# Sparse attention values for two heads at once, and the query norm of cross attention moved into the exponential's scale

## The reference, cut to what matters

```
o_c = softmax(q k_c) v_c                # 31 compressed blocks
o_s = causal_softmax(q k_slc) v_slc     # branch 1
o_w = causal_softmax(q k_win) v_win     # branch 2
o   = g0 * o_c + g1 * o_s + g2 * o_w
```

```
q = rope(rms_norm(p_q, q_norm));  k = rope(rms_norm(p_k, k_norm)), and for the context rms_norm alone
a = softmax(q [k, k_ctx]^T / 8) [v, v_ctx]
rms_norm(x, g) = x / sqrt(mean(x*x) + 1e-6) * g
```

## Time and profile before

| what | value |
| --- | --- |
| median of 3 runs | 3086.56 us (3086.36 to 3092.05) |
| the profiled execution's own time | 3092.79 us |
| its span | 3090.9 us, mean granted TensorE clock 0.952 |
| busy: TensorE, VectorE, ScalarE, GpSimd | 2896.7, 1366.3, 675.4, 1072.2 us |
| the chain that ended last, TensorE's share | 85% (VectorE 5%, DMA 4%) |
| sparse values, L1149 | 640 records, 103.0 us |
| cross attention's scores, L1180 | 128 records, 57.4 us |

### The profile page before, as it was taken

One profiled execution on the slowest core, in us unless ns is written; L12 is line 12 of the kernel. 1 busy time (PEld: TensorE's weight loads), 2 busy tenths in 40 slices (PEclk: granted clock), 3 DMA queues, 4 the chain that ended last, 5 costly groups with the idle time before them and its releaser, 6 DMA issues.

```text
span 3090.9 us, 32580 instructions
## 1 busy us (share of the span) xinstructions
PE 2896.7 (94%) x11791; PEld 1945.3 (63%) x11791; DVE 1366.3 (44%) x2684; ACT 675.4 (22%) x1588; POOL 1072.2 (35%) x574
## 2 busy tenths in 40 slices
PE   7899999999999999998899978989999999999997
PEld 5465544476666644654567546577888544788886
DVE  6333365305455633334655155444355322433464
ACT  2132133123233412323223122111110100211101
POOL 4782583187470007804840000287000583000000
PEclk7999999989999999998898988999999999899998
DMA  7342342253231014312310100254222343122321
GB/s 231 119 126 75 109 126 78 76 154 89 82 89 35 14 55 138 118 61 80 102 47 14 55 14 14 82 158 141 81 92 85 121 152 109 59 91 81 95 86 65
DMA packets 244976, 278.21 MB, mean 90 GB/s; under 512 B 39251, under 2 KB 217696, under 8 KB 244736
## 3 DMA queue, kind: packets, MB, share of 16 engines
q1 hardware_dynamic: 215872, 175.56, 18.6%
q0 software_dynamic: 28224, 100.86, 10.5%
q10 hardware_dynamic: 768, 0.30, 0.0%
HBM read 274.59 MB, written 2.10 MB: 90 GB/s over the span
## 4 chain that ended last, share of the span: by engine, by line
PE 85%; DVE 5%; DMA 4%; issue 2%; ACT 2%; POOL 1%; SPq 1%; DVEq 0%; POOLq 0%; ACTq 0%
PE psum L709 26%; PE psum L1305 24%; PE psum L859 10%; PE psum L845 3%; PE psum L736 3%; PE psum L1149 3%; PE psum L833 2%; PE psum L1135 2%; PE psum L1180 2%; PE psum L751 2%; DMA ring<-in_ffn_w_up 1%; PE psum L983 1%; PE psum L984 1%; DMA ring<-in_ffn_w_gate 1%; ACT probsT L1556 1%
## 5 line engine op out<-in xcount | busy, mean ns | idle before, releaser
L709 PE MATMUL psum<-h,ring 128*128 128x512 f32 (+1 forms) x1808 | 778.5, 589 | 31.7 <-ACT h L1521 24.1
L636 POOL DMA_DIRECT2D ada_ring<-in_ada_w x192 | 114.7, 597 | 1481.6 <-DVE gains L2034 1268.5
L709 PEld LDWEIGHTS psum<-h,ring 128*128 128x128 f32 x1808 | 346.1, 194 | 426.6 <-issue 413.6
L648 POOL TENSOR_SCALAR ada_ring<-ada_ring,cond 128x1024 f32<-128x1024 f32 x168 | 479.6, 2855 | 9.9 <-POOL ada_sum L652 1.8
L652 POOL TENSOR_TENSOR ada_sum<-ada_sum,ada_ring 128x1024 f32<-128x1024 f32 x168 | 398.5, 2372 | 14.9
L859 PE MATMUL psum<-og,ring 128*128 128x512 f32 x768 | 333.2, 593 | 2.3 <-DVE og L2566 2.0
L1305 PE MATMUL psum<-og,arena 128*128 128x256 f32 x1152 | 258.6, 379 | 1.7 <-ACT probs L1872 1.7
L859 PEld LDWEIGHTS psum<-og,ring 128*128 128x128 f32 x768 | 144.6, 190 | 182.0 <-issue 178.5
L1305 PEld LDWEIGHTS psum<-og,arena 128*128 128x128 f32 x1152 | 218.7, 190 | 32.1 <-issue 2.4
L1305 PE MATMUL psum<-h,ring 128*128 128x256 f32 x768 | 180.9, 390 | 4.3 <-ACT h L1521 4.3
L1556 ACT ACTIVATE probsT<-psum 128x128 f32<-128x128 f32 (+3 forms) x232 | 104.3, 450 | 323.6 <-PE psum L833 323.0
(11 more groups left out here) (332 smaller groups left out, 3997.8 us busy)
## 6 DMA issues: line engine op xcount, KB each, us to landing
ada_ring<-in_ada_w POOLq DMA_DIRECT2D x192, 512.0 KB, 4.0
ring<-in_ffn_w_gate SPq DMA_DIRECT2D x22, 1024.0 KB, 5.3
ring<-in_ffn_w_up SPq DMA_DIRECT2D x22, 1024.0 KB, 5.4
ring<-in_ffn_w_down SPq DMA_DIRECT2D x16, 1024.0 KB, 5.0
ring<-in_sc_w_in SPq DMA_DIRECT2D x12, 1024.0 KB, 6.2
ring<-in_mla_w_in SPq DMA_DIRECT2D x10, 1024.0 KB, 6.7
ring<-in_mla_w_out SPq DMA_DIRECT2D x8, 1024.0 KB, 5.1
ring<-in_swa_w_in SPq DMA_DIRECT2D x16, 512.0 KB, 5.2
```

Source lines behind the costliest of these rows:

```text
L636: pool.dma_start(ada_ring[:, i % 2, :], w[k * P:(k + 1) * P, first(part)]).then_inc(arrived[i % 2], n.give(f"ada_in{i % 2}", 16))
L648: step = nc.gpsimd.tensor_scalar(piece, ada_ring[:, i % 2, :], c, None, ALU.mult)
L709: m = pe.matmul(tile.at[:, part], lhs(k), rhs(k), start=(k == 0), stop=(k == K - 1))
```

## The change

Sparse stage: the units' order becomes branch, query block, head. `nsa_v` has 64 columns without zeros, and eight clears of them go. The value step of head 0 only keeps its probability buffer; that of head 1 issues both heads' products, for each key block head 0 and then head 1, each with a 64-column weight and its own half of the output partitions.

Hybrid stage: a query tile is multiplied by the norm's gain twice out of PSUM, once with the cosine (`query_cos`) and once without, for the partner (`take_query`); ScalarE squares the tile in PSUM (`square_query`). TensorE sums the squares with the tokens as rows (`query_sums`), so the sums are 8 columns of 128 partitions; root and reciprocal make them `hy_scale`, with 64 eps in the root, so that the factor 1/8 is in it. It is the scale of the exponential and a factor of the maximum, a column for each unit. The partner of query pair 0 moves ahead of the values, and the wait for the second rotated pair moves into the scores of step 1.

```diff
@@ -218,9 +219,9 @@
-        for e in range(2):
-            for branch in (1, 2):
-                for j in range(TT):
+        for branch in (1, 2):
+            for j in range(TT):
+                for e in range(2):
                     units.append({"branch": branch, "q": j, "head": e, "width": (j + 1) * P, "groups": [(0, (j + 1) * P)],
                                   "opens": False, "first": False, "last": e == 1 and branch == 2 and j == TT - 1,
                                   "blocks": causal_blocks(j), **more})
...
-        nsa_v = [[view(10404 + 1536 * i + 768 * b, TT, 192) for b in range(2)] for i in range(2)]
+        nsa_v = [[view(10404 + 1536 * i + 768 * b, TT, 64) for b in range(2)] for i in range(2)]
...
-                    if u["head"] == 0 and u["branch"] == 1 and u["q"] == 0 and u["pair"] % 2 == 0:
+                    if u["head"] == 0:
+                        first_head.append(pT)
+                        return None
+                    if u["branch"] == 1 and u["q"] == 0 and u["pair"] % 2 == 0:
                         evacuated(value_tiles[kv])
-                    at = 64 - 64 * u["head"]
+                    both = (first_head.pop(), pT)
                     for i, (_, key, q) in enumerate(u["blocks"]):
-                        m = pe.matmul(o[:, q * P:(q + 1) * P], nsa_v[kv % 2][u["branch"] - 1][:, key, at:at + P],
-                                      pT[:, i * P:(i + 1) * P], start=False,
-                                      stop=(u["head"] == 1 and u["branch"] == 2 and i == len(u["blocks"]) - 1),
-                                      skip_group_check=True)
+                        for e in range(2):
+                            m = pe.matmul(o[64 * e:64 * e + 64, q * P:(q + 1) * P], nsa_v[kv % 2][u["branch"] - 1][:, key, :],
+                                          both[e][:, i * P:(i + 1) * P], start=False,
+                                          stop=(u["branch"] == 2 and i == len(u["blocks"]) - 1), skip_group_check=True)
                     return m
...
                 def scores(u, bank):
+                    if u["head"] == 0 and u["q"] == 1:
+                        pe.wait_ge(S["rope_ready"], n.take("rope_ready"))
                     half = slice(64 * (u["head"] % 2), 64 * (u["head"] % 2) + 64)
                     q = hy_q[half, u["head"] // 2, u["q"] * P:(u["q"] + 1) * P]
                     for i in range(2):
...
+                def query_sums(i):
+
+                    tile = next_tile()
+                    pe.wait_ge(S["sq_ready"], n.take("sq_ready"))
+                    squares = sq[:, i, :]
+                    for j in range(TT):
+                        m = pe.matmul(tile.at[:, 2 * j:2 * j + 2], squares[:, j * P:(j + 1) * P], C["ones64"][:, 0:P:64],
+                                      start=True, stop=True)
+                    m.then_inc(S["tile_done"], 1)
...
                     product(w8(open_slot(), 0), h_lat, KT, first_of_slot=True)
-                    head_mean_square(2, lat)
+                    query_sums(0)
+                    partner(2, 1)
                     tokens_tile(open_slot(), 64, range(TT + CT), True)
-                    head_mean_square(3, lat)
-                    partner(2, 2)
-                    partner(3, 1)
-                    for _ in range(3):
+                    query_sums(1)
+                    partner(3, 2)
+                    for _ in range(2):
                         pe.wait_ge(S["rope_ready"], n.take("rope_ready"))
                     attend(units, scores, turned, block_values(lambda u, key: hy_v[:, key, :]), depth=wide)
...
-                        e = nc.scalar.activation(scored, scored, ACT.Exp, bias=neg_max[:, step % 4, g:g + 1], scale=scale,
+                        e = nc.scalar.activation(scored, scored, ACT.Exp, bias=neg_max[:, step % 4, g:g + 1],
+                                                 scale=scale(u) if w > T else scale,
                                                  accum_out=row_sum[:, step % 4, g:g + 1])
...
-                        v = nc.scalar.activation(nsa_v[kv % 2][b][:, :, 64:128],
+                        v = nc.scalar.activation(nsa_v[kv % 2][b],
...
+                def square_query(i):
+                    tile = next_tile()
+                    act.wait_ge(S["head_normed"], n.take("head_normed", 2))
+                    nc.scalar.activation(sq[:, i, :], tile.at, ACT.Square).then_inc(S["sq_ready"], n.give("sq_ready"))
+                    act.wait_ge(S["sq_ready"], n.now("sq_ready"))
+                    act.sem_inc(tile_used[tile.bank], 1)
+
+                def query_root(i):
+                    tile = next_tile()
+                    done(tile)
+                    nc.scalar.activation(hy_scale[:, i, :], tile.at[:, 0:2 * TT], ACT.Sqrt, bias=C["eps64"]
+                                         ).then_inc(tile_used[tile.bank], 1)
...
                     square_head(0, lat)
                     square_head(1, ctx_part)
                     head_rms(0, lat)
-                    square_head(2, lat)
+                    square_query(0)
                     head_rms(1, ctx_part)
                     skip(1)
-                    square_head(3, lat)
-                    head_rms(2, lat)
+                    square_query(1)
+                    query_root(0)
+                    skip(1)
...
-                    head_rms(3, lat)
-                    skip(2)
-                    n.take("head_normed", 2)
-                    attend(units, SCALE64, depth=wide)
+                    query_root(1)
+                    skip(1)
+                    attend(units, lambda u: hy_scale[:, u["head"] // 2, 2 * u["q"] + u["head"] % 2:
+                                                     2 * u["q"] + u["head"] % 2 + 1], depth=wide)
...
-                        nc.vector.tensor_scalar(neg_max[:, b, 0:1], row_max[:, b, 0:1], -scale, None, ALU.mult
+                        nc.vector.tensor_scalar(neg_max[:, b, 0:1], row_max[:, b, 0:1], scale(u), -1.0, ALU.mult, ALU.mult
...
-                        nc.vector.memset(nsa_v[i][b][:, :, 0:64], 0.0)
-                        z = nc.vector.memset(nsa_v[i][b][:, :, 128:192], 0.0)
+                        z = nc.vector.memset(nsa_k[i][b][0:64, 1, :], 0.0)
...
+                def take_query(i):
+
+                    tile = next_tile()
+                    done(tile)
+                    if i:
+                        dve.wait_ge(S["rope_ready"], n.now("rope_ready"))
+                    nc.vector.scalar_tensor_tensor(query_cos[i], tile.at, g_q, C["ax_cos"], ALU.mult, ALU.mult)
+                    nc.vector.tensor_scalar(hy_raw[:, (2 + i) % 3, :], tile.at, g_q, None, ALU.mult
+                                            ).then_inc(S["head_normed"], n.give("head_normed"))
+
+                def query_scale(i):
+
+                    evacuated(next_tile())
+                    nc.vector.reciprocal(hy_scale[:, i, :], hy_scale[:, i, :]).then_inc(S["dve_step"], n.give("dve_step"))
+
+                def turn_query(i):
+
+                    tile = next_tile()
+                    done(tile)
+                    dve.wait_ge(S["dve_step"], n.now("dve_step"))
+                    settle(nc.vector.tensor_tensor(tile.at, tile.at, C["ax_sin"], ALU.mult))
+                    nc.vector.tensor_tensor(hy_q[:, i, :], query_cos[i], tile.at, ALU.add).then_inc(tile_used[tile.bank], 1)
+                    evacuated(tile)
+                    dve.sem_inc(S["rope_ready"], n.give("rope_ready"))
...
                     take_in(0, lat)
                     take_in(1, ctx_part)
                     norm_head(0, lat, g_k)
-                    take_in(2, lat)
+                    take_query(0)
                     norm_head(1, ctx_part, g_k, hy_k[:, T:T + CTX])
                     turn_head(0, hy_k[:, 0:T])
-                    take_in(3, lat)
-                    norm_head(2, lat, g_q)
+                    take_query(1)
+                    query_scale(0)
+                    turn_query(0)
                     skip(1)
-                    norm_head(3, lat, g_q)
-                    turn_head(2, hy_q[:, 0, :])
-                    turn_head(3, hy_q[:, 1, :])
+                    query_scale(1)
+                    turn_query(1)
...
-                    attend(units, SCALE64, None, out, depth=wide)
+                    def scale_of(u):
+                        at = 2 * u["q"] + u["head"] % 2
+                        return hy_scale[:, u["head"] // 2, at:at + 1]
+
+                    attend(units, scale_of, None, out, depth=wide)
```

More of the change, by code:

```diff
@@ L97, in constant_columns @@
         "eps": np.full((P, 1), EPS),
+        "eps64": np.full((P, 1), 64 * EPS),
         "ax_cos": np.cos(ax),
@@ L410, in build @@
         hy_v = view(4352, TT + CT, P)
+        hy_scale = view(5120, 2, 2 * TT)
         ctx_tok = view(8704, CT, D)
@@ L1083, in nsa @@
                     hidden = tile
-                keys, value_tiles = {}, {}
+                keys, value_tiles, first_head = {}, {}, []
```

(11 more changed lines are left out.)

## The result

The changed kernel takes 3071.26 us (median of 20 runs, 3060.34 to 3086.57); the kernel before, over 20 runs, 3092.07 us. The ratio is 0.9933, 95% interval 0.992 to 0.9946: 20.8 us faster. I had forecast 38 us and a range that ended at 3070.

The account below looks back on a forecast made before the run. It took TensorE as the bound in both stages, with a VectorE chain before cross attention's scores; 25.7 us sparse plus 12.7 cross attention, 38 together, gave 3048.6 us, 8-in-10 range 3030 to 3070.

Parts of the forecast that it names:

- The couples: Sparse stage values: two heads' 64-column products overlap in different column halves, 1.14 us saved per branch and pair, 18.2 us.
- The waits: Sparse stage: fewer TensorE waits for copies of transposed probabilities, 0.9 us per eight units without a projection, 7.5 us saved.
- Rival 1: Sparse stage: copies and softmax do not shrink, so waits cost 8 us instead of saving 7.5; 3064 us, chance 0.20.
- The loads: Sparse stage: value copies and loads keep number and order, weight slots open at the same points; no effect.
- The memsets: Sparse stage: eight VectorE memsets removed, worth nothing, since VectorE waits 25.90 us after them.
- The chain before the scores: Cross attention: shorter VectorE work between token projection and first row maximum, saving 5.9 us in turn 2, 7.7 in turn 1.
- The two bank waits: Cross attention, before the token projection: TensorE waits for query tiles' banks, 1.3 us more and 1.1 us.
- The exponential: Cross attention: scale as a column adds 0.09 us in each of 32 strictly serial steps, 2.9 us lost.
- TensorE's clock: Cross attention: with the shorter gap, part of the lower-clock loss goes, 1 us a turn (bounds 0 and 2.7), 2 saved.
- the prediction's own signs of being wrong: Three signs: couples over 0.15 us, copy waits beyond 3 us per eight units, token projection ending more than 6 us later.
- a rival for the sparse stage: No change: the sparse stage idles oftener and TensorE's clock falls in many pairs, 1.7 us a fall; chance 0.04.
- The base: Whole kernel: the median of 3086.56 us from which the 38 us were subtracted to give 3048.6.

Follow-up runs that it names:

- order_only: Kernel before with only the sparse stage's new unit order, old 128-column value weights kept: 3080.16 us, ratio 0.9946.
- busy_all: Changed kernel with thrown-away 512-column products ahead of each early partner product and of each turn's first transposes: 3056.79 us, ratio 0.9876.
- sparse_only: Kernel before with only the sparse stage's part of the change, cross attention as before: 3072.66 us, ratio 0.9923.
- cross_wide: Kernel before with only cross attention's part of the change, query sums over 128 columns instead of 2: 3079.65 us, ratio 0.995.
- late_bank: Kernel with only the sparse part changed, plus two more copies of each query tile before the one freeing its bank: 3095.80 us, ratio 0.9998.
- after_again: The changed kernel once more, unaltered, for a second profile and its spread: 3074.05 us, ratio 0.9926.
- cross_only: Kernel before with only cross attention's part of the change, sparse attention as before: 3099.55 us, ratio 1.001.
- wide_sums: Changed kernel with the query sums over 128 columns (same sums repeated) instead of 2: 3057.52 us, ratio 0.9873.
- serial_halves: Kernel before with only the sparse part, each value step issuing all blocks of head 0, then all of head 1: 3080.78 us, ratio 0.9944.
- after: The changed kernel itself, both parts, against the kernel before: 3071.26 us, ratio 0.9933.
- wide_busy: Changed kernel with 128-column query sums and thrown-away products in TensorE's three waits of each turn: 3055.71 us, ratio 0.9877.

## Why the prediction was wrong, point by point

- **The couples (18.2 us): the mechanism held, the term was too large for the stage.** Eight records take 0.58 us as read from the earlier trace rows. In the last pair the difference to order_only is 13.14 - 11.79 = 1.35 us for eight units, more than the 1.14 that I had priced. Over the stage it is less: 543.4 us in order_only, 530.2 to 532.9 in eight profiles of the full sparse part and 536.8 in a ninth, so 10 to 13 us, and 7 by the ninth. The "up to two-fold" that the prediction quotes from the Trainium skill, page TensorEngine Tiling (Array Packing), stands there in the section Theoretical Speedup; here sixteen records take 1.51 us in one half and 1.02 as couples, with what going in and out costs.
- **The waits (7.5 us): too small for the stage.** The order alone gives 13.5 us of stage, 13.8 in the median. In the last pair it saves only 13.80 - 13.14 = 0.66 us of each eight units, so most of it lies where projections stand between the steps, and there I had put the gain at nothing. Which waits it takes away there is not traced. Couples and waits together were 25.7 us, against 24.0 to 26.8 measured in the stage (20.2 in busy_all): a right sum of two wrong sizes, which is luck. Eight units were forecast at 11.7 us and take 11.79. Rival 1 (the chain takes it back) fell.
- **The loads (nothing): wrong by some 4 us.** The prediction kept the weight loads at nothing because their number and order stay. But the layer behind the sparse stage takes 262.9 to 264.4 us in the four kernels with the old value products, and in the ten with 64-column ones 262.8 and 263.1 us in two and 266.4 to 270.1 in eight (medians 263.8 and 268.0). TensorE comes there earlier and waits for weights, and the 12 records behind the wait are slower too; the layer's mean granted clock is 0.99 before and 0.97 after. Timeline of TensorE, before and then after:

```profile
1222.44 5.42 PE L709 MATMUL psum<-arena,ring 128*128 128x512 f32 x12 [1.17 <-DMA ring<-in_mla_w_q_b]
```

```profile
1206.12 6.94 PE L711 MATMUL psum<-arena,ring 128*128 128x512 f32 x12 [3.54 <-DMA ring<-in_mla_w_q_b]
```

  Of the 24 to 27 us that the sparse stage gains, 21.9 arrive in the median of sparse_only. What sets the time of this load is not traced. The memsets were nothing, as said; no run tested them alone.
- **The chain before the scores (5.9 + 7.7): right where the clock holds.** 4.1 us instead of 3.6 from projection to first maximum. The two bank waits that I priced at 1.3 more and 1.1 us are 1.84 (before 0.44, so 1.4 more) and 1.48. In turn 2 the projection ends 3.7 us later, as forecast (3.6), and 9.0 us are saved behind it: 5.4 us, forecast 5.9. cross_wide, with the chain unchanged, gives 14 to 15 us.
- **The exponential (+2.9): wrong.** The instruction does take 0.09 us more, and by the Trainium skill, page ScalarE: Activation LUTs, section What ACT_TABLE_LOAD costs, each column operand adds about 93 ns, with which the trace agrees (964 against 875). But my sentence that each step runs strictly one after the other left out TensorE. Its step of 3.67 us is longer than the chain's 3.48.
- **TensorE's clock (a gain of 2 us, 1 a turn with bounds 0 and 2.7): the step that failed.** I asked whether a shorter gap would let the old slow steps recover, and not what the two waits that I had just added would do; a loss was not within the bounds. The waits, with the 2-column records, stand right before the token projection, and the clock falls there in some executions: in 5 of 8 turns profiled with the 2-column sums and no filler, in none of the 18 profiled turns of the other kernels outside late_bank. (In one more of the eight, turn 1 of after_again, it fell behind the first wait, where a product took 8.73 us instead of 7.03, and was back before the projection.) A projection at 0.50 costs 9 us, and 2.5 more pass until the first maximum. In turn 2 of after_again the projection ends 12.6 us later than before the change, counted from the last maximum of turn 1, which was one of the prediction's own signs of being wrong (more than 6). That takes back the whole gain of the cross part, 12.7 us forecast and nothing measured in cross_only. The gain of 2 us itself did not come either: from first to 16th maximum the turns take 57.8 and 57.2 us before, 61.8 and 57.0 after, 57.0 and 58.0 in cross_wide. I had named the fall after a 2.10 us wait in a rival for the sparse stage, where it did not grow: the granted clock over its 405 us is 0.98 before and after.
- **The base.** 5.5 us of the 22.7 by which I missed the time come from the median of three runs that I subtracted from; in the gain the miss is 17 us, of which 12.7 are the cross part and 3.8 the sparse part (25.7 forecast, 21.9 in sparse_only).

## What to carry to other kernels

Price a wait of TensorE not by its length alone: ask what stands right behind it. Waits of 1.4 to 2 us ahead of a stretch of small products cost 9 us here each time the clock fell, and a wider product that computes the same sums several times over cost 0.1 us and won 14. Ask of a stage made faster whether the next stage's weights are there when it ends: here about 4 us went to that. And time the parts apart when a change has two: one carried all of the gain, the other hid its own. The version to use is wide_sums (3057.5 us, 0.9873), as fast as any here within the intervals and without filler products.

## What the runs showed of the hardware beyond that

- 2-column and 128-column fp32 products with a 128-column weight took nearly the same time, 8 records in 0.95 and 1.05 us. Behind them the projection was slow in 5 of 8 turns with 2 columns (no filler), and in none of 6 with 128.
- fp32 products with 64-column weights in the same column half followed each other at 0.094 us a record (serial_halves, 16 in 1.51 us), and couples in two halves at 0.064 (after, 16 in 1.02), each with the way in and out; so overlapping was worth 1.5-fold, not two-fold.
- With the clock kept, the attention of a turn takes 54.5 us from first to 16th maximum (wide_busy, both turns), and 56.8 to 61.8 in the kernels without filler in the attention.
- Executions of the kernel before spread over 14 to 27 us in one call, those of the changed kernel over 26 us in 20 and 35 in 7, those of busy_all over 7 us in 6. In the two profiles of the changed kernel the cross attention layer differs by 13 us through the clock, and the layer behind the sparse stage by 6 the other way.
